# Hybrid retention / MoBA decoder step on one core: the second norm's squares are added on GpSimd before TensorE sums them, and GpSimd's drains give way to semaphore counts

## The chip, the core and the metric

The kernel runs on one core of a Trainium2 chip. A core has TensorE (PE in the profile; PEld is its loading of weights), VectorE (DVE), ScalarE (ACT), GpSimd (POOL), SyncE (SP, which here only issues DMAs) and 16 DMA engines that fill one on-chip memory (SBUF). The metric is the time of one execution on the device in microseconds (us); lower is better.

## The reference, cut to what matters

One decoder layer is applied to a prompt of 512 tokens and to a decoding group of 8 sequences with 4 new tokens each. Model width is 1024, that is 8 tiles of 128 features. All is float32.

```python
h = _rmsnorm(x, norm1_w) * (1 + sc1) + sh1
z = h @ w_in                      # 3584 columns: retention q k v gate, MoBA q k v
...                               # retention and block-sparse attention
x = x + g1 * (concat([ret_out, moba_out]) @ w_out)
h2 = _rmsnorm(x, norm2_w) * (1 + sc2) + sh2     # _rmsnorm: x * rsqrt(mean(x*x) + eps) * w
x = x + g2 * ((silu(h2 @ w_gate) * (h2 @ w_up)) @ w_down)
```

The change touches the second norm of the prompt, whose mean runs over the 1024 features of each token, and the rotary rotation (`x1*cos - x2*sin`, `x1*sin + x2*cos`) of retention queries and keys. The sample group's block-sparse attention reads 8 x 32 pages of cached keys (K) and values (V), 128 rows of 512 numbers each; this is most of the memory traffic and is spread over the whole kernel.

## The kernel before, in words

Every engine has its own hand-written program; they meet at counting semaphores (`s_...`). The work is laid out in numbered slots. Slot `s` holds one group of four pages of the sample's attention, and beside it one piece of the prompt's work.

In slot `s` TensorE first multiplies the turned keys of group `s` with the queries (`keys`, L1161), then does the prompt's piece, then weighs the values of group `s - 12` (`weigh`, L1216). The keys take this way: GpSimd gathers 1 MB of K with an indirect DMA (`gather`, L523) into one of two buffers; VectorE turns it (`turn_keys`, L1846, written KT) when the buffer has arrived and TensorE has used the turned keys before; TensorE uses it in the next slot. `gather(g)` waits until the group `g - 2` is turned, because it takes that buffer. Values come by four DMAs of 256 KB a group, issued by SyncE (L410), into two rings of four buffers; each waits until TensorE has used its buffer.

Slots 13 to 29 hold the last input tiles. There GpSimd also rotates the eight tiles of retention keys and queries (`rotate`, L548, L549, L551): tile `m` at turn `g = m + 4` of its loop, right behind `gather(g)`.

Slots 43 to 50 (`R_OUT + f`, f = 0 to 7) are the ones that the change is about. Output projection tile `f` is 24 matmuls (L1128, L1129, L1130: every product of float32 numbers is made of three rounded ones). For them ScalarE rounds the weights (`split_out`, L658, written whi) and VectorE takes the rest (L1809, written rawlo). When tile `f - 1` is done, VectorE adds it to x (`residual`, L2126), makes the product with the norm's weight (`gained`, L2131), takes `rawlo` for tile `f + 1` (L1809) and turns the next keys (L1846), in this order. ScalarE squares the new x (L950; L961 for the last tile) into one of two buffers `stage`. TensorE sums these squares over the features with a column of ones: `sum_squares(k)`, four matmuls of one column, behind the output tile of the next slot. Four numbers a partition accumulate in PSUM over all eight k, after a product with zeros that clears them (L1548).

In slot 48 VectorE also takes the sums and maxima of a sequence's logits, TensorE forms the gates (`block_gates`, L1180), and VectorE selects the blocks in slot 49 (`select`, L1872 to L1889), ahead of that slot's residual. TensorE's next use of it is `turn_max` (L1184) in slot 49's tail, ahead of the keys of slot 50.

Slot 51 (`R_NORM`) and the two behind it are the norm: VectorE takes the reciprocal (L2160), ScalarE the root, VectorE puts it on four diagonals (L2164), TensorE spreads it over the partitions (L1578), VectorE copies it to `rb` (L2168), GpSimd scales the eight tiles (`scale_x`, L566), ScalarE rounds them (L970), VectorE takes the rest (L2152). Then the feed-forward tiles begin (slot 54 on), and behind slot 64 the sample's own output projection and feed-forward go between them.

GpSimd's program at loop turn `g` is: wait for the turned keys, `gather(g)`, then what that turn holds. At turns 46 and 47 it rotates the sample's queries and keys (`rotate_half`, L532, L533, L535), at turn 48 it masks two blocks of keys (`masked_k`, L541), at turns 54 and 55 it scales the tiles. Between operations that depend on each other it drains its pipe: `pool.drain()`, L534 and L536 in `rotate_half`, L550 and L552 in `rotate`.

Of the kernel before, what the change touches and what calls it, by code (L numbers as in the profile page):

```python
# [7 lines left out]
ALU, ACT, AX = mybir.AluOpType, mybir.ActivationFunctionType, mybir.AxisListType  # L8

P = 128  # L10
# [6 lines left out]
HP = H // 2  # L17
# [9 lines left out]
KT = DM // P  # L27
# [122 lines left out]
def decoder_step(nc, x_prompt, x_sample, cache_k, cache_v, state_ret, page_table, c_prompt, c_sample,  # L150
# [7 lines left out]
    def sem(name):  # L158
        return persist.enter_context(nc.semaphore(name))
# [168 lines left out]
    s_hn, s_sg = sem("heads_normed"), sem("gate_silu")  # L328
    s_kst, s_kss = sem("k_v_prompt_stored"), sem("k_v_sample_stored")

    s_srot, s_srs, s_ssg = sem("s_rotated"), sem("s_rstd"), sem("s_gate_silu")

# [17 lines left out]
    s_le, s_to = sem("logits_kept"), sem("own_probsT_copied")  # L352

    s_sqx, s_ssm, s_r1, s_r2 = sem("x2_squares"), sem("x2_sums"), sem("x2_inverse"), sem("x2_rstd")
    s_nx, s_gmt = sem("x2_scaled"), sem("gmod_turned")

    RINV, RDIAG, RSPREAD = 1, 2, 3
    s_xr, s_x2s, s_x2q, s_x2i = sem("x2T_ready"), sem("x2s_ready"), sem("x2s_squares"), sem("x2s_inverse")
# [161 lines left out]
    def _(pool):  # L520
# [4 lines left out]
        def rotate_half(n, half, op):  # L525
            ta = kmask[0][:, 0:256].rearrange("p (h d) -> p h d", h=H)
            tb = kmask[1][:, 0:256].rearrange("p (h d) -> p h d", h=H)
            cos = C("cos_s").unsqueeze(1).broadcast_to((S, H, 32))
            sin = C("sin_s").unsqueeze(1).broadcast_to((S, H, 32))
            z = zs[:, n * W:(n + 1) * W].rearrange("p (h c d) -> p h c d", h=H, c=2)  # L530
            o = (qrs, krs)[n][:, :].rearrange("p (h c d) -> p h c d", h=H, c=2)
            pool.tensor_tensor(ta, z[:, :, half, :], cos, ALU.mult)  # L532
            pool.tensor_tensor(tb, z[:, :, 1 - half, :], sin, ALU.mult)  # L533
            pool.drain()  # L534
            pool.tensor_tensor(o[:, :, half, :], ta, tb, op)  # L535
            pool.drain()  # L536

        def masked_k(b):
            if b >= 2:
# [4 lines left out]
        def rotate(m):  # L544

            z, other = zT[:, Z_OF[m], :], swapped[:, m % 2, :]
            pool.wait_ge(s_swap[m % 2], 64 * ((m - M_TURN) // 2 + 1))
            pool.tensor_tensor(other, other, C("sin"), ALU.mult)  # L548
            pool.tensor_tensor(z, z, C("cos"), ALU.mult)  # L549
            pool.drain()  # L550
            pool.tensor_tensor(z, z, other, ALU.add)  # L551
            pool.drain().then_inc(s_rk, 1)  # L552

        def queries_decayed(hp):
            if hp == 0:
# [6 lines left out]
        def scale_x(k):  # L562

            if k == 0:
                pool.wait_ge(s_r1, RSPREAD)
            pool.tensor_tensor(zT[:, k, :], zT[:, k, :], rb[:, :], ALU.mult).then_inc(s_nx, 1)  # L566

        def scale_heads(hp):
            pool.wait_ge(s_hrs, hp + 2)
# [7 lines left out]
        for g in range(2, NG):  # L577
            pool.wait_ge(s_kt, g - 1)
            gather(g)
            if M_TURN <= g - 4 < M_TURN + 2 * HP:  # L580
                if g - 4 == M_TURN:
                    pool.wait_ge(s_const, 32)
                rotate(g - 4)
            if g > R_PAIR and (g - R_PAIR - 2) % 3 == 0 and g <= R_PAIR + 11:
                queries_decayed((g - R_PAIR - 2) // 3)
            if g in (R_PAIR + 7, R_PAIR + 10, R_PAIR + 13):
                scale_heads((g - R_PAIR - 7) // 3)
            if g == R_PAIR + 3:
                pool.wait_ge(s_hrs, 1)
                heads = mobatok.rearrange("p i (h d) -> p i h d", h=H)  # L590
                pool.tensor_tensor(heads, heads, gain[:, 4:8, 0:8].unsqueeze(3).broadcast_to((P, TT, H, HD)), ALU.mult).then_inc(s_hm, 1)
            if g in (R_NORM + 3, R_NORM + 4):
                for k in range(4):
                    scale_x(4 * (g - R_NORM - 3) + k)
            if g == R_OUT + 3:
                pool.wait_ge(s_sev, NIN + 2)
                pool.wait_ge(s_xx, KT)
                pool.wait_ge(s_const, 64)
                rotate_half(0, 0, ALU.subtract)
                rotate_half(0, 1, ALU.add)  # L600
            if g == R_OUT + 4:
                rotate_half(1, 0, ALU.subtract)
                rotate_half(1, 1, ALU.add)
                pool.sem_inc(s_srot, 1)
            if g == R_OUT + 5:
                masked_k(0)
                masked_k(1)
            if g == R_SAMPLE + 5:
                pool.wait_ge(s_rpe, SO)
                pool.tensor_tensor(state[:, :, :, :], state[:, :, :, :],  # L610
                                   C("c_dec_s").unsqueeze(1).unsqueeze(3).broadcast_to((P, NB_SEQ, HP, HD)), ALU.mult).then_inc(s_sdc, 1)
            if R_SAMPLE + 6 <= g < R_SAMPLE + 9:
                b = 2 * (g - R_SAMPLE - 5)
                masked_k(b)
                masked_k(b + 1)

    @block.scalar
    def _(act):
# [319 lines left out]
        for f in range(KT):  # L938
# [6 lines left out]
                split_out(f + 1)  # L945
            if f >= 1:
                act.wait_ge(s_ev, F_OUT + f + 2)
                if f >= 3:
                    act.wait_ge(s_ssm, f - 2)
                act.activation(stage[(f - 1) % 2][:, :], x2T[:, f - 1, :], ACT.Square).then_inc(s_sqx, 1)  # L950
            if f == KT - 1:
                exps(B_NORM)
            if f:
# [3 lines left out]

        act.activation(st2[:, 28:29], C("eps"), ACT.Sqrt)
        act.wait_ge(s_ev, F_OUT + KT + 2)
        act.wait_ge(s_ssm, KT - 2)  # L960
        act.activation(stage[1][:, :], x2T[:, KT - 1, :], ACT.Square).then_inc(s_sqx, 1)  # L961
        slot(R_NORM)
        next_chunk(5)
# [20 lines left out]
        def sample_slot(s):  # L984
# [4 lines left out]
            if s == R_SAMPLE + 8:  # L989
                act.wait_ge(s_sts, NB_SEQ // 2)  # L990
                act.dma_start(ret_sample[0].rearrange("b (hp h2) d v -> (h2 d) b hp v", h2=2), state[:, :, :, :]).then_inc(s_state, 16)
                act.wait_ge(s_srot, 1)
                act.dma_start(x2s[:, :], x_sample.rearrange("b t d -> (b t) d")).then_inc(s_xs, 16)
            if s == S_END + 1:
                act.wait_ge(s_ofs, 1)
# [67 lines left out]
    def _(pe):  # L1063
# [479 lines left out]

        def sum_squares(k):
            if k == 0:
                pe.matmul(DB[:, 0:TT], ident, C("pad0")[:, 0:TT], start=True, stop=False, skip_group_check=True)  # L1548
            pe.wait_ge(s_sqx, k + 1)
            for i in range(TT):  # L1550
                last = pe.matmul(DB[:, i:i + 1], stage[k % 2][:, i * P:(i + 1) * P], ones[:, 0:1], start=False, stop=(k == KT - 1),
                                 skip_group_check=True)
            last.then_inc(s_ssm, 1)

        for f in range(KT):
            slot_head(R_OUT + f)
# [7 lines left out]
                 last_in=(lambda: turn_heads(3)) if f == 0 else None)  # L1564
            if f == KT - 1:
                slot_head(R_NORM)
            if f:
                sum_squares(f - 1)
            if f == KT - 1:
                turn_probs(B_NORM, 0)  # L1570
                sum_squares(KT - 1)
            slot_rest(R_OUT + f)


# [40 lines left out]
        def sample_slot(s):  # L1615

            if s == R_SAMPLE:
                pe.wait_ge(s_srot, 1)
                for n, x in enumerate((qrs, krs)):
                    for j in range(HP):  # L1620
                        last = pe.transpose(SB[:, (n * HP + j) * S:(n * HP + j + 1) * S], x[:, j * P:(j + 1) * P], ident[0:S, 0:S])
# [104 lines left out]
    def _(dve):  # L1726
# [429 lines left out]
        residual(KT - 1, 16 + KT - 1, bank[(KT - 1) % 2])  # L2156
        gained(KT - 1)
        turn_half_keys(R_NORM + 1, 0)
        dve.wait_ge(s_ssm, KT)
        then(ts(st2[:, 8:12], DB[:, 0:TT], 1.0 / DM, EPS, ALU.mult, ALU.add))  # L2160
        dve.reciprocal(st2[:, 8:12], st2[:, 8:12]).then_inc(s_r1, 1)
        dve.wait_ge(s_r2, 1)
# [1 line left out]
            last = ts(stage[0][:, i * P:(i + 1) * P], ident, st2[:, i:i + 1], None, ALU.mult)  # L2164
        last.then_inc(s_r1, 1)
        turn_half_keys(R_NORM + 1, 1)
        dve.wait_ge(s_ssm, KT + 1)
        cp(rb[:, :], DB[:, :]).then_inc(s_r1, 1)  # L2168
        slot_head(R_NORM + 1)
        slot_rest(R_NORM + 1)  # L2170
# [238 lines left out]
```

## Time and profile before

| what | value |
|---|---|
| median of 3 runs | 1039.15 us (1037.05 to 1048.32) |
| profiled execution, its own time | 1034.07 us |
| its span, first to last instruction | 1032.2 us |
| TensorE's mean granted clock | 0.976 |
| TensorE busy | 961.6 us, 93% |
| VectorE, ScalarE, GpSimd busy | 624.5, 338.4, 139.4 us |
| DMA | 269.14 MB, mean 261 GB/s |

The profile is of one execution; its time is 5.1 us below the median of the three runs, and 1.9 us above its span. Busy shares are means over stages with different limits. DMA-issuing, semaphore and drain instructions are not counted as busy.

### The profile page before, as it was taken

What the parts mean: (1) busy time and instruction counts of PE and PEld (TensorE: products, weight loads), DVE (VectorE), ACT (ScalarE), POOL (GpSimd) and SP (SyncE); (2) the same over time, 40 slices, a digit from 0 to 9 for tenths busy, and PEclk for the clock granted to TensorE, in tenths of its full rate; (3) what the DMA queues carried; (4) which work ended last, traced back from release to release, by engine and by line L of the source; (5) the groups of instructions that cost most, each with busy time, mean ns of one, the idle gap of its engine ahead of it and who ended that gap; (6) DMA issues with size and microseconds to landing.
All of it is one profiled execution on the core that took longest, in us unless ns stands there. A gap on an engine that the chain in (4) does not pass through costs nothing.

```text
span 1032.2 us, 20974 instructions
## 1 busy us (share of the span) xinstructions
PE 961.6 (93%) x7919; PEld 675.8 (65%) x7919; DVE 624.5 (60%) x1067; ACT 338.4 (33%) x735; POOL 139.4 (14%) x129
## 2 busy tenths in 40 slices
PE   3879998999999987979989999999999999999996
PEld 2557775766666644547756767676777777777775
DVE  1566874677767667876788584432655555453244
ACT  5412233334333624542252152332333222121113
POOL 0011111444210132204151220000000000000000
PEclk9899999999999989999989899999999999999998
DMA  9978877999786889988998668778476988787652
GB/s 340 364 257 282 284 252 268 296 274 300 255 287 215 276 320 390 356 288 280 362 320 285 231 230 265 230 228 267 144 218 167 240 226 231 218 251 248 204 194 87
DMA packets 217973, 269.14 MB, mean 261 GB/s; under 512 B 13473, under 2 KB 168425, under 8 KB 209682
## 3 DMA queue, kind: packets, MB, share of 16 engines
q1 hardware_dynamic: 110226, 126.65, 38.7%
q10 hardware_dynamic: 98432, 74.04, 23.6%
q0 software_dynamic: 9216, 67.11, 17.7%
q8 instruction: 63, 1.03, 0.4%
q14 instruction: 36, 0.29, 0.1%
HBM read 260.04 MB, written 5.64 MB: 257 GB/s over the span
## 4 chain that ended last, share of the span: by engine, by line
PE 72%; DVE 8%; DMA 7%; issue 5%; SPq 4%; DVEq 2%; ACT 1%; POOLq 1%; POOL 1%; ACTq 0%
PE banks L1128 13%; PE banks L1129 12%; PE banks L1130 12%; PE banks L1078 6%; PE banks L1216 4%; PE banks L1141 4%; PE banks L1143 4%; PE banks L1142 4%; PE banks L1161 4%; DVE KT L1846 3%; DMA V<-in_cache_v 3%; DMA K<-in_cache_k,kidx 1%; SPq L420 1%; PE banks L1340 1%; DMA early<-in_w_mod 1%
## 5 line engine op out<-in xcount | busy, mean ns | idle before, releaser
L658 ACT ACTIVATE whi<-raw 128x1024 fp32r<-128x1024 f32 (+1 forms) x76 | 78.6, 1035 | 298.0 <-PE banks L1130 144.4
L1128 PE MATMUL banks<-ahi,whi 128*128 128x512 f32 x416 | 169.2, 407 | 0.1
L1846 DVE STREAM_TRANSPOSE KT<-K 128x2048 f32<-128x2048 f32 x63 | 145.5, 2310 | 30.0 <-DMA K<-in_cache_k,kidx 15.1
L1129 PE MATMUL banks<-alo,whi 128*128 128x512 f32 x416 | 163.5, 393 | 0.0
L1130 PE MATMUL banks<-ahi,rawlo 128*128 128x512 f32 x416 | 163.3, 393 | 0.0
L1809 DVE TENSOR_TENSOR rawlo<-raw,whi 128x1024 fp32r<-128x1024 f32 (+1 forms) x76 | 91.3, 1201 | 54.3 <-ACT whi L658 51.2
L523 POOL DMA_INDIRECT K<-in_cache_k,kidx x64 | 64.0, 1000 | 412.4 <-DVE KT L1846 363.7
L1128 PEld LDWEIGHTS banks<-ahi,whi 128*128 128x128 f32 x416 | 78.7, 189 | 31.2 <-issue 13.1
L1141 PE MATMUL banks<-ahi,whi 128*128 128x512 f32 x216 | 90.2, 417 | 1.2 <-DVE rawlo L1816 0.9
L1130 PEld LDWEIGHTS banks<-ahi,rawlo 128*128 128x128 f32 x416 | 78.8, 189 | 17.3
L1161 PE MATMUL banks<-KT,qbd 128*32 128x128 f32 x2048 | 74.0, 283 | 15.7 <-DVE KT L1846 13.0
L1129 PEld LDWEIGHTS banks<-alo,whi 128*128 128x128 f32 x416 | 78.8, 189 | 14.9
L1143 PE MATMUL banks<-ahi,rawlo 128*128 128x512 f32 x216 | 85.1, 394 | 0.0
L1142 PE MATMUL banks<-alo,whi 128*128 128x512 f32 x216 | 84.9, 393 | 0.0
L1161 PEld LDWEIGHTS banks<-KT,qbd 128*32 128x32 f32 x2048 | 56.7, 112 | 29.7 <-issue 14.1
L1216 PE MATMUL banks<-V,pT 128*32 128x512 f32 x368 | 64.4, 630 | 11.5 <-DMA V<-in_cache_v 11.4
L1816 DVE TENSOR_TENSOR rawlo<-raw,whi 128x1024 fp32r<-128x1024 f32 x28 | 35.8, 1279 | 30.4 <-ACT whi L651 14.9
L1141 PEld LDWEIGHTS banks<-ahi,whi 128*128 128x128 f32 x216 | 40.9, 190 | 17.9 <-issue 7.5
L748 ACT ACTIVATE pm<-banks,st 128x128 f32<-128x128 f32 (+3 forms) x32 | 16.6, 524 | 96.8 <-DVE st L1989 91.4
L1143 PEld LDWEIGHTS banks<-ahi,rawlo 128*128 128x128 f32 x216 | 40.8, 189 | 9.4
L1142 PEld LDWEIGHTS banks<-alo,whi 128*128 128x128 f32 x216 | 41.1, 190 | 7.3
L1750 DVE TENSOR_TENSOR xtmp<-xtmp,banks 32x256 f32<-32x256 f32 x90 | 37.5, 417 | 7.1 <-issue 0.4
(330 smaller groups left out, 1462.1 us busy)
## 6 DMA issues: line engine op xcount, KB each, us to landing
V<-in_cache_v SPq DMA_DIRECT2D x184, 256.0 KB
rawm<-in_w_mod ACTq DMA_DIRECT2D x14, 1024.0 KB
raw<-in_w_in ACTq DMA_DIRECT2D x12, 1024.0 KB
zT<-in_cache_v SPq DMA_DIRECT2D x48, 256.0 KB
raw<-in_w_gate ACTq DMA_DIRECT2D x22, 512.0 KB
raw<-in_w_up ACTq DMA_DIRECT2D x22, 512.0 KB
srw<-in_w_gate SPq DMA_DIRECT2D x22, 512.0 KB, 5.6
srw<-in_w_up SPq DMA_DIRECT2D x22, 512.0 KB, 7.3
```

The lines of the kernel that those rows point to most:

```text
L523: pool.indirect_dma_start(Kb[g % 2][:, :], None, ck, bass.IndirectOffsetOnAxis(kidx[:, g:g + 1], 0)).then_inc(s_k[g % 2], 16)
L658: act.activation(whi[t % 2][:, 0:kd, :], raw[u][:, 0:kd, t % 2 * P:(t % 2 + 1) * P], ACT.Copy).then_inc(s_hi, 1)
L1128: pe.matmul(out[:, :], whi[t % 2][:, k, :], hi(k), start=(first and n == 0), stop=False)
L1129: pe.matmul(out[:, :], whi[t % 2][:, k, :], lo(k), start=False, stop=False)
L1130: last = pe.matmul(out[:, :], low[:, k, :], hi(k), start=False, stop=(final and n == kd - 1))
L1141: pe.matmul(DB[:, :], whi[m % 2][:, k, :], ahi[:, k, :], start=(k == 0), stop=False)
L1142: pe.matmul(DB[:, :], whi[m % 2][:, k, :], alo[:, k, :], start=False, stop=False)
L1143: last = pe.matmul(DB[:, :], wlow[:, k, :], ahi[:, k, :], start=False, stop=(k == KT - 1))
L1161: last = pe.matmul(LG[32 * gq:32 * gq + 32, (g % 4) * P:(g % 4 + 1) * P], qbd[g // NGRP % 2][:, j, :], KTb[:, :, j, :], start=(jj == 0), s ...
L1216: pe.matmul(VO[32 * pg:32 * pg + 32, :], pT[:, n, 32 * pg:32 * pg + 32], bufs[pg][:, :], start=(n == 0), stop=(n == NGRP - 1)).then_inc(s_ ...
L1809: tt(rawlo[u][:, 0:kd, cols], raw[u][:, 0:kd, cols], whi[t % 2][:, 0:kd, :].bitcast(F32), ALU.subtract).then_inc(s_lo, 1)
L1846: dve.transpose(KTb[:, :, :, :], Kb[g % 2][:, :]).then_inc(s_kt, 1)
```

## The change

GpSimd gets a new function, `add_squares(k)`. ScalarE writes the first tile's squares straight into `rb` and the others into `stage` in turn; GpSimd adds tiles 1 to 6 to `rb`, at its loop turns 47 to 52, behind the gather of that turn and ahead of the rotations and masks. TensorE sums twice in all, at the end of slot 50: `rb`, and the last tile's squares. ScalarE's waits for a free `stage` are now for GpSimd (`s_sqa`) and no longer for TensorE (`s_ssm`). In `rotate`, `rotate_half` and before `masked_k` the drains are gone; the operations count one semaphore up (`s_srot`, and `s_rk` from the last operation itself) and GpSimd waits for its count.

```diff
-            pool.tensor_tensor(ta, z[:, :, half, :], cos, ALU.mult)
-            pool.tensor_tensor(tb, z[:, :, 1 - half, :], sin, ALU.mult)
-            pool.drain()
-            pool.tensor_tensor(o[:, :, half, :], ta, tb, op)
-            pool.drain()
+            done = 4 * HP + 3 * (2 * n + half)
+            pool.wait_ge(s_srot, done)
+            pool.tensor_tensor(ta, z[:, :, half, :], cos, ALU.mult).then_inc(s_srot, 1)
+            pool.tensor_tensor(tb, z[:, :, 1 - half, :], sin, ALU.mult).then_inc(s_srot, 1)
+            pool.wait_ge(s_srot, done + 2)
+            pool.tensor_tensor(o[:, :, half, :], ta, tb, op).then_inc(s_srot, 1)
...
-            pool.tensor_tensor(other, other, C("sin"), ALU.mult)
-            pool.tensor_tensor(z, z, C("cos"), ALU.mult)
-            pool.drain()
-            pool.tensor_tensor(z, z, other, ALU.add)
-            pool.drain().then_inc(s_rk, 1)
+            pool.tensor_tensor(other, other, C("sin"), ALU.mult).then_inc(s_srot, 1)
+            pool.tensor_tensor(z, z, C("cos"), ALU.mult).then_inc(s_srot, 1)
+            pool.wait_ge(s_srot, 2 * (m - M_TURN + 1))
+            pool.tensor_tensor(z, z, other, ALU.add).then_inc(s_rk, 1)
...
+        def add_squares(k):
+            pool.wait_ge(s_sqx, k + 1)
+            if k > 1:
+                pool.wait_ge(s_sqa, k - 1)
+            pool.tensor_tensor(rb[:, :], rb[:, :], stage[k % 2][:, :], ALU.add).then_inc(s_sqa, 1)
...
+            if 1 <= g - R_OUT - 3 < KT - 1:
+                add_squares(g - R_OUT - 3)
...
             if g == R_OUT + 5:
+                pool.wait_ge(s_srot, 4 * HP + 12)
                 masked_k(0)
                 masked_k(1)
...
-                if f >= 3:
-                    act.wait_ge(s_ssm, f - 2)
-                act.activation(stage[(f - 1) % 2][:, :], x2T[:, f - 1, :], ACT.Square).then_inc(s_sqx, 1)
+                if f >= 4:
+                    act.wait_ge(s_sqa, f - 3)
+                act.activation(rb[:, :] if f == 1 else stage[(f - 1) % 2][:, :], x2T[:, f - 1, :], ACT.Square).then_inc(s_sqx, 1)
...
-        def sum_squares(k):
-            if k == 0:
-                pe.matmul(DB[:, 0:TT], ident, C("pad0")[:, 0:TT], start=True, stop=False, skip_group_check=True)
-            pe.wait_ge(s_sqx, k + 1)
+        def sum_over_features(src, final):
             for i in range(TT):
-                last = pe.matmul(DB[:, i:i + 1], stage[k % 2][:, i * P:(i + 1) * P], ones[:, 0:1], start=False, stop=(k == KT - 1),
-                                 skip_group_check=True)
-            last.then_inc(s_ssm, 1)
+                last = pe.matmul(DB[:, i:i + 1], src[:, i * P:(i + 1) * P], ones[:, 0:1], start=False, stop=final, skip_group_check=True)
+            return last
+
+        def sum_squares():
+
+            pe.matmul(DB[:, 0:TT], ident, C("pad0")[:, 0:TT], start=True, stop=False, skip_group_check=True)
+            pe.wait_ge(s_sqa, KT - 2)
+            sum_over_features(rb, False)
+            pe.wait_ge(s_sqx, KT)
+            sum_over_features(stage[1], True).then_inc(s_ssm, 1)
...
             if f == KT - 1:
                 slot_head(R_NORM)
-            if f:
-                sum_squares(f - 1)
             if f == KT - 1:
                 turn_probs(B_NORM, 0)
-                sum_squares(KT - 1)
+                sum_squares()
```

The other edits renumber waits to fit: the last square waits for `s_sqa >= 5`, VectorE for `s_ssm` 1 and 2, and TensorE's and ScalarE's waits for the rotated sample rows are now `s_srot >= 28`.

## Rows read from the trace of the kernel before

**Rows 1.** The page, part 1: busy time, share of the span and instructions.

```profile
PE 961.6 (93%) x7919; PEld 675.8 (65%) x7919; DVE 624.5 (60%) x1067; ACT 338.4 (33%) x735; POOL 139.4 (14%) x129
```

**Rows 2.** Busy time by window (start:end us, length; engines; clock; DMA share; GB/s).

```profile
503.00:512.00 9.00, 9.00 (x76) 6.92 (x76) 5.73 (x19) 1.06 (x1) 0.94 (x1) 1.00 1.00 346
...
531.00:545.00 14.00, 9.80 (x81) 4.37 (x73) 13.76 (x12) 7.28 (x13) 11.53 (x10) 0.76 1.04 388
```

**Rows 3.** Line L1551, all instructions: count, min/median/max ns, first and last start.

```profile
L1551 PE MATMUL banks<-ct,stage x64: 164/250/271, 470.5 to 527.2; 128*128 128x1 f32 x64
```

**Rows 4.** TensorE's instructions in order of time (start, length, then what).

```profile
479.51 0.95 PE L1551 MATMUL banks<-ct,stage 128*128 128x1 f32 x8
480.38 1.07 PE L1216 MATMUL banks<-zT,pT 128*32 128x512 f32 x8
```

**Rows 5.** The chain that ended last, 451 to 500 us (start, length, what).

```profile
477.67 7.83 issue
...
489.52 6.85 DMA K<-in_cache_k,kidx
...
496.40 2.32 DVE KT L1846
...
498.85 1.08 PE banks L1161 x32
```

**Rows 6.** GpSimd's instructions in order of time, around the sample's rotations.

```profile
475.05 1.16 POOL L523 DMA_INDIRECT K<-in_cache_k,kidx  x1 [0.78 <-issue]
...
476.92 0.74 POOL L533 TENSOR_TENSOR kmask<-zs,cts 32x256 f32<-32x256 f32 x1
485.53 0.73 POOL L535 TENSOR_TENSOR krs<-kmask,kmask 32x256 f32<-32x256 f32 x1 [7.86 <-issue]
```

**Rows 7.** VectorE's instructions in order of time, slots 45 to 49.

```profile
467.77 2.30 DVE L1846 STREAM_TRANSPOSE KT<-K 128x2048 f32<-128x2048 f32 x1
...
485.38 2.31 DVE L1846 STREAM_TRANSPOSE KT<-K 128x2048 f32<-128x2048 f32 x1 [1.02 <-DMA K<-in_cache_k,kidx]
...
513.18 1.22 DVE L1809 TENSOR_TENSOR rawlo<-raw,whi 128x1024 fp32r<-128x1024 f32 x1
514.32 2.31 DVE L1846 STREAM_TRANSPOSE KT<-K 128x2048 f32<-128x2048 f32 x1
```

**Rows 8.** TensorE's instructions in order of time, slots 47 to 50.

```profile
497.64 1.07 PE L1216 MATMUL banks<-zT,pT 128*32 128x512 f32 x8
...
508.09 0.39 PE L1180 MATMUL banks<-sm,ct 128*128 128x16 f32 x2
...
516.87 0.27 PE L1184 MATMUL banks<-ct,sm 128*1 128x128 f32 x1
517.07 1.08 PE L1161 MATMUL banks<-KT,qbd 128*32 128x128 f32 x32
```

**Rows 9.** ScalarE's instructions in order of time: the square of tile 5.

```profile
512.72 0.64 ACT L950 ACTIVATE stage<-x2T 128x512 f32<-128x512 f32 x1 [4.12 <-DVE x2T L2126]
```

**Rows 10.** Line L566, all instructions: GpSimd's operation on one tile of 128x512.

```profile
L566 POOL TENSOR_TENSOR zT<-zT,rb x8: 1259/1268/1280, 531.4 to 541.5; 128x512 f32<-128x512 f32 x8
```

**Rows 11.** ScalarE in order of time: the first tile rounded behind GpSimd's scaling.

```profile
532.71 0.72 ACT L970 ACTIVATE ahi<-zT,mT 128x512 fp32r<-128x512 f32 x1 [3.94 <-POOL zT L566]
```

**Rows 12.** In order of time, VectorE and GpSimd: operations that overlap, near 252 us.

```profile
251.97 1.91 DVE L1816 TENSOR_TENSOR rawlo<-raw,whi 128x1024 fp32r<-128x1024 f32 x1 [2.32 <-ACT whi L651]
...
252.76 2.25 POOL L549 TENSOR_TENSOR zT<-zT,ctr 128x512 f32<-128x512 f32 x1
```

**Rows 13.** GpSimd in order of time: the first rotation of a prompt tile.

```profile
182.84 1.28 POOL L551 TENSOR_TENSOR zT<-zT,swapped 128x512 f32<-128x512 f32 x1 [1.55 <-issue]
```

**Rows 14.** TensorE in order of time, the norm's slots: values awaited, first feed-forward matmul.

```profile
534.50 2.45 PE L1216 MATMUL banks<-V,pT 128*32 128x512 f32 x4 [2.41 <-DMA V<-in_cache_v]
...
544.58 0.50 PE L1128 MATMUL banks<-ahi,whi 128*128 128x512 f32 x1
```

**Rows 15.** Line L2152, all instructions: VectorE's rest of the eight scaled tiles.

```profile
L2152 DVE SCALAR_TENSOR_TENSOR alo<-zT,mT,ahi x8: 737/740/5524, 535.2 to 545.9; 128x512 fp32r<-128x512 f32 x8
```

More of the change, by code:

```diff
@@ L329, in decoder_step @@
     s_kst, s_kss = sem("k_v_prompt_stored"), sem("k_v_sample_stored")
-    s_srot, s_srs, s_ssg = sem("s_rotated"), sem("s_rstd"), sem("s_gate_silu")
+    s_srot, s_srs, s_ssg = sem("rotation_steps"), sem("s_rstd"), sem("s_gate_silu")
     s_rpe, s_rdve = sem("s_retention_on_pe"), sem("s_retention_on_dve")
@@ L354, in decoder_step @@
     s_sqx, s_ssm, s_r1, s_r2 = sem("x2_squares"), sem("x2_sums"), sem("x2_inverse"), sem("x2_rstd")
-    s_nx, s_gmt = sem("x2_scaled"), sem("gmod_turned")
+    s_nx, s_gmt, s_sqa = sem("x2_scaled"), sem("gmod_turned"), sem("x2_squares_added")
     RINV, RDIAG, RSPREAD = 1, 2, 3
@@ L603, in _ @@
                 rotate_half(1, 1, ALU.add)
-                pool.sem_inc(s_srot, 1)
             if g == R_OUT + 5:
+                pool.wait_ge(s_srot, 4 * HP + 12)
                 masked_k(0)
@@ L959, in _ @@
         act.wait_ge(s_ev, F_OUT + KT + 2)
-        act.wait_ge(s_ssm, KT - 2)
+        act.wait_ge(s_sqa, KT - 3)
         act.activation(stage[1][:, :], x2T[:, KT - 1, :], ACT.Square).then_inc(s_sqx, 1)
@@ L991, in sample_slot @@
                 act.dma_start(ret_sample[0].rearrange("b (hp h2) d v -> (h2 d) b hp v", h2=2), state[:, :, :, :]).then_inc(s_state, 16)
-                act.wait_ge(s_srot, 1)
+                act.wait_ge(s_srot, 4 * HP + 12)
                 act.dma_start(x2s[:, :], x_sample.rearrange("b t d -> (b t) d")).then_inc(s_xs, 16)
@@ L1617, in sample_slot @@
             if s == R_SAMPLE:
-                pe.wait_ge(s_srot, 1)
+                pe.wait_ge(s_srot, 4 * HP + 12)
                 for n, x in enumerate((qrs, krs)):
@@ L2158, in _ @@
         turn_half_keys(R_NORM + 1, 0)
-        dve.wait_ge(s_ssm, KT)
+        dve.wait_ge(s_ssm, 1)
         then(ts(st2[:, 8:12], DB[:, 0:TT], 1.0 / DM, EPS, ALU.mult, ALU.add))
@@ L2166, in _ @@
         turn_half_keys(R_NORM + 1, 1)
-        dve.wait_ge(s_ssm, KT + 1)
+        dve.wait_ge(s_ssm, 2)
         cp(rb[:, :], DB[:, :]).then_inc(s_r1, 1)
```

## The prediction

> **What bounds the kernel now.** I read the page first. TensorE is busy 93% of the span, VectorE 60%, GpSimd 14% [rows 1]. Such a kernel gets shorter by what leaves TensorE, as long as nothing else comes late, and the page cannot say whether something does. So I went to the stretch that the change touches, slots 44 to 51 (about 464 to 531 us), by windows. From 503 to 512 us TensorE is busy for the whole of 9.00 us at a granted clock of 1.00 [rows 2]. The same row shows the DMA engines at a share of 1.00 and 346 GB/s, so they are the second candidate. Behind the norm it is different: from 531 to 545 us TensorE works 9.80 of 14.00 us, its mean granted clock is 0.76, and the DMA share is 1.04 [rows 2].
>
> Then the chain that ended last. Just where TensorE is full, this chain runs over GpSimd: 7.83 us of "issue", then a gather's transfer of 6.85 us, the turning of its keys, and at 498.85 us TensorE's keys [rows 5]. GpSimd's own timeline tells what that "issue" is: between L533 at 476.92 us and L535 at 485.53 us stands only the drain L534, 7.86 us long [rows 6]. VectorE's wait for the preceding gather (issued 475.05 us) ends at 485.38 us [rows 7]. So in this trace the drain ends when the outstanding gather lands. A chain says who was last, not by how much: before the keys at 498.85 us TensorE's previous group starts at 497.64 us and takes 1.07 us [rows 8], which leaves 0.14 us. Both paths are almost equally long there.
>
> **The sums on TensorE.** L1551 has 64 records, 8 for each of 8 groups [rows 3]. Busy times overlap, so I take start to start: the group at 479.51 us is followed by the values at 480.38 us, 0.87 us [rows 4]. Six of eight groups go: 6 x 0.87 = 5.22 us, all on the engine that is full. The clearing product moves from the first to the last group, and nets to nothing. At the end of slot 50 there are two sums as before, in a slightly different order around the turned probabilities, so the way from the last tile to the norm is not shortened. All the gain must come from slots 44 to 49.
>
> **The drains of the sample's rotations.** Without them, gather 47 can go when group 45 is turned, at 467.77 + 2.30 = 470.07 us [rows 7], and not at 475.05 us; gathers 48 and 49 move up by more, since 7.86 us of drain lie behind the first. Their keys stop being late, which is worth the 0.14 us above, and keeps this path from being the next bound when TensorE gets faster: with the drains left, the 3.5 us of the first four groups would be lost against it. The new waits count GpSimd's own operations. They could hang on the outstanding gather like the drains, or cost next to nothing. ScalarE's first rounding starts at 532.71 us [rows 11], 0.05 us after the first scaling (531.4 + 1.26 us [rows 10]) ended, with a gather issued just ahead of it; so an operation's count comes at once. I take 0; the other end is a rival.
>
> **The drains of the prompt's rotations.** The first has 1.55 us of drain before L551 [rows 13], and there are two a tile. Sixteen at up to 1.55 us are 25 us of GpSimd, which is 14% busy [rows 1]. That idle time is the cover: the rotated tiles are needed slots later, and a gather mostly waits for turned keys longer than for this. Were the cover gone, a gather would come up to 3.1 us later in each of eight slots. I take 0, since no stretch of the chain that I read there runs over these drains.
>
> **The additions on GpSimd.** Six operations of 128x512, 1.27 us each by the nearest operation of that size [rows 10], 7.6 us of an engine with room. ScalarE's new waits are for additions at least a slot old: 0. The wait that counts is on GpSimd: `add_squares(k)` waits for the square of tile k, and behind it in GpSimd's queue stand the rotations, the masks and the next gather. For tile 5 the square ends at 512.72 + 0.64 = 513.36 us [rows 9], so the addition ends near 514.7 us. The next gather waits for a group of keys whose turning begins at 514.32 us and takes 2.31 us [rows 7]. So the gather's own condition comes 2 us later, and the addition delays nothing. In slot 50 tile 6's square gives the same order. I take 0, up to 0.5 us a slot if ScalarE were late.
>
> **Contention with VectorE.** The addition starts when VectorE does `rawlo`, which is on the way to the next turned keys. Near 252 us such a pair overlaps: `rawlo` takes 1.91 us and GpSimd's product 2.25 us, and not about 1.22 and 1.28 us [rows 7, 10, 12]. So they hold each other. For tile 5, `rawlo` starts at 513.18 us, 0.18 us ahead of the square's end; then GpSimd is the one that waits, and it has time. In slot 50 `exp_bias` comes between and the addition may be first, which costs up to 1.27 us in that slot. Bounds: 0, and 1.27 us in each of the three last slots (3.8 us). I take 0.2 us, near the lower end, since five of six slots have the order of tile 5.
>
> The Trainium skill (SBUF — State Buffer, "Who interferes with whom") says that a VectorE instruction with two SBUF inputs contends with a GpSimd instruction that reads SBUF, and that the first to issue holds the port for its whole length. The trace agrees. The rule speaks against this change; with GpSimd first in every slot it gives the slow rival below.
>
> **What is late next.** TensorE gains 0.87 us a slot only while keys are ready. The tight place is slot 50: from `block_gates` at 508.09 us to the keys at 517.07 us TensorE takes 8.98 us [rows 8], 8.11 us without the sum. VectorE starts on the gates' result and has turned the keys at 514.32 + 2.31 = 516.63 us, 8.54 us after the same point, and 0.14 us more pass until TensorE uses them (as at 498.71 to 498.85 us [rows 5]): 8.68 us. So 8.68 - 8.11 = 0.57 us are given back. I found no second place so tight, with slot 51's keys next.
>
> **The sum.** -5.22 - 0.14 + 0.57 + 0.2 = -4.6 us. Behind the norm each load starts upon a use by TensorE, so the whole pattern shifts earlier, waits included. Against the profiled execution: 1034.07 - 4.6 = 1029.5 us. The median of the runs is 5.1 us above that execution, so against it 1034.5 us. The measurement tells about 1% (10.4 us) from no change; this is 0.4%.
>
> **The rivals.**
>
> *The transfers absorb it.* With the DMA share at 1.00 [rows 2] a faster TensorE may only wait for bytes. For: 346 to 388 GB/s in these windows. Against: a slot moves 2.5 MB (1 of K, 1 of V, half a weight chunk of 1), which in a slot of 8.11 us is 308 GB/s, below the 388 GB/s of the second row of [rows 2]. If it held, gain 0: 1039.2 us.
>
> *More is gained at the norm.* The first feed-forward matmul, at 544.58 us, waits behind values (2.41 us at 534.50 us [rows 14]). VectorE's last rest starts at 545.9 us and takes 0.74 us [rows 15], 546.6 us, and is needed only by the last three of 24 matmuls. Slot 49's 8.98 us less gates, keys, sum, values and turned maximum (0.3, 1.0, 0.9, 1.0, 0.2) leave 5.6 us for a tile, so 21 matmuls take 4.9 us, and a start at 541.7 us would do. If earlier gathers clear the queues, up to 2.9 us more: 1031.6 us. Against: those values are requested upon TensorE's use, also after the change.
>
> *GpSimd first, slower than before.* In every slot the addition starts ahead of `rawlo` and holds it 1.27 us, keys follow late, and 7.6 us are paid against 5.36 gained: +7.6 + 0.57 - 5.36 = +2.8 us, 1042.0 us. It decides once the uncovered hold is over (5.36 - 0.57) / 6 = 0.8 us a slot. Against: the order at 513 us, and the idle time that VectorE has in most slots (5.73 us busy of 9.00 [rows 2]).
>
> *The stall stays.* The change doesn't free GpSimd, because its counts too wait for the gather. Then the four first groups' 3.5 us and an addition's 1.27 us are lost on the way to gather 48: -4.6 + 3.5 + 1.3 = about 0, 1039.3 us. Against: rows 11.
>
> **How the numbers follow.** Forecast 0.60, absorbed 0.12, more at the norm 0.13, GpSimd first 0.10, stall 0.05. The forecast's own range is 1032 to 1038.5 us (no contention; contention at its upper bound). The range must take in the slow rival at 1042 and the better one, and three runs before spread from 1037.05 to 1048.32 us, so medians move by a few us: 1029 to 1042 us. No case reaches 1% by its terms; faster by over 1% gets 0.06 (the norm's waits shrinking with a better clock), slower by over 1% 0.04, within 1% 0.90.
>
> **What would show it.** Right: L1551's successor has 16 records; no "issue" over 1 us before L535; gather 48 issued before 480 us; slots 44 to 49 shorter by about 0.87 us each save one, where the keys of slot 50 wait for VectorE some 0.5 us; first feed-forward matmul 4.6 us earlier. Wrong: `rawlo` at 2 us or more in these slots, additions that end after the turned keys, or new waits for K, V or weights between 464 and 531 us.

## The result, and the profile after

The changed kernel takes 1045.2 us (median of 20 runs, 1042.3 to 1049.76), the kernel before 1040.59 us (20 runs, 1034.26 to 1049.24). The measured ratio is 1.0052, with a 95% interval of 1.0032 to 1.0073. That is 5.4 us slower (the two medians alone differ by 4.6 us), and not 4.6 us faster. It is within 1%, and 1045.2 us is above the end of my range (1042 us).

The two profiled executions stand at opposite ends of their spreads: that of before took 1034.07 us, less than any of the 20 runs, that of after 1049.76 us, the longest of its 20 (span 1047.9 us). Already at the keys of slot 44, ahead of the second norm's part of the change, they are 9.7 us apart (463.73 and 473.41 us). So I compare stretches from one TensorE landmark to the next, and no absolute times.

The page, part 1, of after; it answers to [rows 1]:

```profile
PE 961.3 (92%) x7871; PEld 672.0 (64%) x7871; DVE 624.7 (60%) x1067; ACT 338.3 (32%) x735; POOL 152.3 (15%) x135
```

48 matmuls are gone and six GpSimd operations have come, as meant. GpSimd in order of time, after, slots 44 to 49; it answers to [rows 6]:

```profile
480.56 0.98 POOL L525 DMA_INDIRECT K<-in_cache_k,kidx  x1 [0.38 <-DVE KT L1859]
483.44 1.81 POOL L575 TENSOR_TENSOR rb<-rb,stage 128x512 f32<-128x512 f32 x1 [1.91 <-ACT stage L961]
485.21 0.73 POOL L536 TENSOR_TENSOR kmask<-zs,cts 32x256 f32<-32x256 f32 x1
485.91 0.72 POOL L537 TENSOR_TENSOR kmask<-zs,cts 32x256 f32<-32x256 f32 x1
486.72 0.73 POOL L539 TENSOR_TENSOR krs<-kmask,kmask 32x256 f32<-32x256 f32 x1
...
489.89 0.98 POOL L525 DMA_INDIRECT K<-in_cache_k,kidx  x1 [0.16 <-issue]
...
495.53 0.98 POOL L525 DMA_INDIRECT K<-in_cache_k,kidx  x1 [0.16 <-issue]
...
502.83 0.95 POOL L525 DMA_INDIRECT K<-in_cache_k,kidx  x1 [1.33 <-DVE KT L1859]
```

The "issue" of 7.86 us ahead of `krs` is gone: the second of its products (L537) ends at 486.63 us and L539 starts at 486.72 us. In after the trace has no landing for the gather issued at 480.56 us, but in e9, a second profile of the same kernel, the same gather goes at 479.25 us and lands 9.5 us later, at 488.7 us, while the first L539 for `krs` starts at 485.41 us. So the counts don't wait for the gather. From gather 46 (473.54 us here, 463.85 us before) to gather 48 it takes 16.35 us, and before 25.67 us. Up to here all goes as predicted, and TensorE takes it up: its keys start as follows, in order of time (the last two are those of slots 48 and 49):

```profile
481.54 1.06 PE L1172 MATMUL banks<-KT,qbd 128*32 128x128 f32 x32
...
489.56 1.08 PE L1172 MATMUL banks<-KT,qbd 128*32 128x128 f32 x32
...
504.80 1.26 PE L1172 MATMUL banks<-KT,qbd 128*32 128x128 f32 x32
512.08 1.07 PE L1227 MATMUL banks<-V,pT 128*32 128x512 f32 x8
520.57 0.61 PE L1191 MATMUL banks<-sm,ct 128*128 128x16 f32 x2 [7.43 <-DVEq L1880]
521.11 1.94 PE L1172 MATMUL banks<-KT,qbd 128*32 128x128 f32 x32
```

From the keys of slot 44 to those of slot 48 (473.41 to 504.80 us) it takes 31.39 us, and before 35.12 us: 3.73 us gained. The next slot takes 16.31 us, and before 9.56 us. TensorE ends its values at 513.15 us and stands for 7.43 us until the gates can be taken. The chain that ended last, after, 495 to 522 us, says why:

```profile
496.36 17.00 DMA raw<-in_w_out
...
513.38 1.06 ACT whi L669
...
514.64 3.27 DVEq L1874
517.91 1.10 DVE sm L1872
519.01 1.12 DVE sm L1873
```

The last chunk of `w_out` (1 MB, the weights of tiles 6 and 7) is 17.00 us under way. ScalarE, which rounds it, and VectorE, which takes its rest ahead of everything else, each in order of time:

```profile
496.36 0.39 ACTq L831 DMA_DIRECT2D raw<-in_w_out  x1
...
513.38 1.06 ACT L669 ACTIVATE whi<-raw 128x1024 fp32r<-128x1024 f32 x1 [13.60 <-DMA raw<-in_w_out]
```

```profile
514.47 1.23 DVE L1822 TENSOR_TENSOR rawlo<-raw,whi 128x1024 fp32r<-128x1024 f32 x1 [9.11 <-ACT whi L669]
515.61 2.31 DVE L1859 STREAM_TRANSPOSE KT<-K 128x2048 f32<-128x2048 f32 x1
517.84 1.18 DVE L1872 TENSOR_REDUCE sm<-lgs 128x8 f32<-128x1024 f32 x1
```

One late load holds three things that don't need it: VectorE works in its written order, so behind `rawlo` stand the turning of keys (gathered from 495.53 us on; in e9 this gather landed in 8.9 us) and both reductions for the gates, and behind these TensorE. In the kernel before, this chunk was issued at 488.53 us and its rounding began at 497.03 us, released by TensorE and not by the load: it was there within 8.5 us.

The windows of after and of before (start:end, length, busy times as in [rows 2], granted clock, DMA share, GB/s):

```profile
486.00:508.00 22.00, 22.00 (x230) 16.07 (x229) 13.26 (x21) 3.87 (x5) 12.72 (x12) 1.00 1.05 368
508.00:514.00 6.00, 5.14 (x27) 3.23 (x25) 0.00 (x0) 0.62 (x1) 0.00 (x0) 1.00 0.81 309
514.00:522.00 8.00, 1.43 (x22) 1.33 (x26) 6.58 (x10) 1.90 (x3) 2.74 (x2) 0.62 0.94 305
```

```profile
486.00:508.00 22.00, 21.75 (x206) 16.54 (x204) 16.12 (x22) 4.33 (x6) 8.32 (x10) 1.00 0.93 342
```

The DMA engines are full for 22 us on end (a share of 1.05), and the rate over the same 22 us rises from 342 to 368 GB/s. The last row of after shows a second price: behind the stop the granted clock is 0.62, a mean of the two levels 1.2 and 2.4 GHz, and the keys at 521.11 us take 1.94 us and not 1.08. The following slot, 521.11 to 531.33 us, takes 10.22 us, and the same slot before took 8.66 us.

The view of DMA issues, after and before (queue, count, KB of a descriptor or a load, median us from issue to landing); both loads go through ScalarE's queue, the state's first:

```profile
state<-in_state_ret ACTq DMA_DIRECT2D x1, 0.2 KB, 17.8
```

```profile
state<-in_state_ret ACTq DMA_DIRECT2D x1, 0.2 KB, 11.8
```

The state (1 MB, issued at 480.83 us) lands at 498.6 us, 2.2 us after the chunk was issued behind it; before, it was issued at 471.17 and landed at 483.0 us, 5.5 us ahead of the chunk.

### The profile page after: what moved, and what is told of

The parts are those of the page before. It is cut to its first block, busy times and chain, and to the rows that moved or that the text cites. A ratio compares the mean times of both kernels' runs of the same rounds, so it can differ in the third digit from the quotient of the medians.

```text
span 1047.9 us, 20865 instructions
## 1 busy us (share of the span) xinstructions
PE 961.3 (92%) x7871; PEld 672.0 (64%) x7871; DVE 624.7 (60%) x1067; ACT 338.3 (32%) x735; POOL 152.3 (15%) x135
## 4 chain that ended last, share of the span: by engine, by line
PE 69%; DMA 12%; DVE 10%; SPq 2%; issue 2%; DVEq 2%; ACT 1%; ACTq 0%; POOLq 0%
PE banks L1139 14%; PE banks L1140 12%; PE banks L1141 12%; PE banks L1089 6%; PE banks L1227 5%; DMA V<-in_cache_v 4%; DVE KT L1859 4%; PE banks L1152 4%; PE banks L1172 4%; DMA K<-in_cache_k,kidx 3%; PE banks L1154 3%; PE banks L1153 3%; DMA early<-in_w_mod 2%; DMA raw<-in_w_out 2%; PE banks L1351 1%
## 5 line engine op out<-in xcount | busy, mean ns | idle before, releaser
L1227 PE MATMUL banks<-V,pT 128*32 128x512 f32 x368 | 67.5, 643 | 16.7 <-DMA V<-in_cache_v 16.7
```

What stands on the lines that cost most here:

```text
L1227: pe.matmul(VO[32 * pg:32 * pg + 32, :], pT[:, n, 32 * pg:32 * pg + 32], bufs[pg][:, :], start=(n == 0), stop=(n == NGRP - 1)).then_inc(s_ ...
```

## The experiments

Each kernel has 12 runs. They fall into three groups (e1 to e4, e5 to e8, e9 to e12), each with 35 runs of the kernel before on the same chip (medians 1038.57, 1040.07 and 1040.22 us), and the ratios are against these. The table gives what I read from each profile, in us. "Chunk" is the last one of `w_out`, from issue to its rounding; with a "<" its landing was earlier, since TensorE released the rounding (where the trace has that landing, it is 5.0 us after the issue in e3 and 5.6 us in e7). "State" is from issue to landing; "moved" where it is loaded later. The last time column runs from the keys of slot 44 to the first feed-forward matmul.

| kernel | keys 44 to 48 | 48 to 49 | chunk | state | 44 to feed-forward | ratio (95%) |
|---|---|---|---|---|---|---|
| before | 35.12 | 9.56 | < 8.5 | 11.8 | 80.85 | 1 |
| changed | 31.39 | 16.31 | 17.0 | 17.8 | 86.85 | 1.0052 (1.0032 to 1.0073) |
| e9, changed again | 31.37 | 16.82 | 17.5 | 18.2 | 84.48 | 1.0051 (1.0022 to 1.008) |
| e1, additions only | 37.35 | 10.98 | < 8.1 | 15.8 | 83.24 | 1.0022 (0.9992 to 1.0052) |
| e2, sample's counts only | 34.76 | 9.14 | 11.3 | 19.6 | 81.83 | 1.0022 (0.9997 to 1.0048) |
| e3, prompt's counts only | 35.47 | 9.19 | < 8.5 | 11.0 | 81.42 | 0.9992 (0.9967 to 1.0018) |
| e4, gather 49 held | 31.37 | 15.05 | 10.4 | 17.5 | 82.47 | 1.0037 (1.0014 to 1.006) |
| e5, state later | 31.37 | 9.67 | 10.6 | moved | 75.60 | 0.9988 (0.9956 to 1.0019) |
| e6, before, state later | 34.78 | 10.76 | 13.2 | moved | 82.07 | 1.0008 (0.9978 to 1.0037) |
| e7, before, six sums out | 36.69 | 11.09 | < 9.0 | 16.2 | 83.24 | 1.0038 (1.0005 to 1.0072) |
| e8, before, additions on top | 35.69 | 9.16 | < 8.5 | 12.5 | 81.21 | 1.0016 (0.9987 to 1.0045) |
| e10, e5 again | 31.41 | 8.37 | < 7.7 | moved | 74.65 | 0.9989 (0.996 to 1.0019) |
| e11, values held | 31.36 | 10.48 | 10.5 | 19.0 | 78.13 | 1.0004 (0.9974 to 1.0033) |
| e12, both | 31.38 | 9.17 | 9.3 | moved | 76.30 | 0.9966 (0.9939 to 0.9993) |

### The parts of the change, each alone

**e1: the additions, with all drains back.** Against the changed kernel:

```diff
...
-            pool.wait_ge(s_srot, done + 2)
-            pool.tensor_tensor(o[:, :, half, :], ta, tb, op).then_inc(s_srot, 1)
+            pool.drain()
+            pool.tensor_tensor(o[:, :, half, :], ta, tb, op)
+            pool.drain()
```

and the same in `rotate`.

> The additions on GpSimd and the two sums on TensorE as in the change; all drains as before. Collision theory (the sample's rotations without drains send gathers 48 to 50 early, into the load of w_out's last chunk, which then takes 17.0 us and stops TensorE for 7.4 us): without that, no stop; gathers 47 to 49 are late as before, so most of the six sums' 5.2 us is lost against them: ratio 0.997 to 1.001. Additions theory (waits and port contention of the additions cost the time): ratio 1.004 or more, as in the full change. Prompt theory (the counts in the prompt's rotations cost it, upstream): ratio below 1.000.

1042.83 us. With TensorE faster the gathers are late, each engine in order of time (GpSimd, VectorE, TensorE):

```profile
485.44 0.73 POOL L535 TENSOR_TENSOR kmask<-zs,cts 32x256 f32<-32x256 f32 x1
492.44 0.73 POOL L537 TENSOR_TENSOR krs<-kmask,kmask 32x256 f32<-32x256 f32 x1 [6.28 <-issue]
...
496.42 0.98 POOL L525 DMA_INDIRECT K<-in_cache_k,kidx  x1 [0.80 <-issue]
```

```profile
505.30 2.31 DVE L1859 STREAM_TRANSPOSE KT<-K 128x2048 f32<-128x2048 f32 x1 [4.31 <-DMA K<-in_cache_k,kidx]
```

```profile
507.76 1.93 PE L1172 MATMUL banks<-KT,qbd 128*32 128x128 f32 x32 [5.34 <-DVE KT L1859]
```

The gather behind the drains takes 8.9 us to land (6.85 us in [rows 5]), and TensorE stands for 5.34 us. So the time that TensorE gave up comes back as this wait, and more: 37.35 us against 35.12. The chunk is in time here. The ratio of 1.0022 lies between the two theories, above the 1.001 of the one and below the 1.004 of the other, and its interval touches both; it is the trace that tells the late gathers from a cost of the additions.

**e2: the counts of the sample's rotations alone.** Against before, only `rotate_half` and the waits for it take the change's form, with 3 counts a half and 12 in all.

> Only the sample's rotations (rotate_half) get counts in place of drains; sums, additions and the prompt's rotations as before. Collision theory: the gathers go early and the load of w_out's last chunk takes over 12 us to land, with nothing gained on TensorE: slower, ratio 1.005 to 1.010, and an idle time of several us on TensorE in slot 48 or 49. Additions theory: 1.000. Prompt theory: 1.000.

1041.03 us. The gathers go early, the state takes 19.6 us, and the rounding of the chunk is the first that waits for the load. ScalarE in order of time:

```profile
504.50 1.06 ACT L659 ACTIVATE whi<-raw 128x1024 fp32r<-128x1024 f32 x1 [7.06 <-DMA raw<-in_w_out]
```

It starts 11.3 us after the issue at 493.24 us, and TensorE, still with its sums to do, has no wait in slot 48 or 49. So the expectation was too hard: the chunk took less than 12 us, there was no idle time, and the ratio is 1.0022 and not 1.005 or more. Taking the drains away thus moved the lateness from K to the weights and the state, ahead of any gain.

**e3: the counts of the prompt's rotations alone.** Against before, only `rotate` takes the change's form.

> Only the prompt's rotations (rotate) get counts in place of drains. Collision theory and additions theory: nothing, ratio 0.999 to 1.001; the 4 to 5 us by which the changed kernel's profile is late from slot 17 to 24 are the spread between executions. Prompt theory: ratio 1.003 to 1.005, and the same lag from slot 17 on in the profile.

1039.23 us, ratio 0.9992: nothing, as predicted for this part. Its profile does lag from slot 15 on (keys at 195.4 us, before 189.9 us), but so do e1, e6, e7 and e8, which keep these drains (193.8 to 195.4 us); the lag is no mark of the counts. It is the one profile of before that is early.

**e8: the additions on top of before.** TensorE's eight sums stay; GpSimd does the six additions as well, and ScalarE waits for both.

```diff
+            if 1 <= g - R_OUT - 3 < KT - 1:
+                add_squares(g - R_OUT - 3)
...
                     act.wait_ge(s_ssm, f - 2)
+                    act.wait_ge(s_sqa, f - 2)
```

> The kernel before with all eight groups of sums on TensorE, and the six additions on GpSimd besides (their result is not used). All drains as before. Transfer theory: the additions are free but for the turns behind the drains, up to 2.6 us at gather 48 and 49, ratio 1.000 to 1.003. Additions theory: 1.004 or more.

1039.97 us, ratio 1.0016; the stretch to the feed-forward differs by 0.4 us. The additions as such cost nothing that these runs resolve.

**e7: the first six sums left out of before, and nothing in their place.**

```diff
         def sum_squares(k):
-            if k == 0:
+            if k == KT - 2:
                 pe.matmul(DB[:, 0:TT], ident, C("pad0")[:, 0:TT], start=True, stop=False, skip_group_check=True)
...
-            if f:
+            if f == KT - 1:
                 sum_squares(f - 1)
```

> The kernel before with the first six groups of sums left out and nothing in their place: the norm's mean misses six of eight tiles. No additions; all drains as before. Transfer theory: TensorE's 5.2 us are turned into waits for keys or weights in slots 47 to 49, ratio 0.999 to 1.003. Additions theory: the full 5 us appear, ratio 0.995 to 0.997.

1043.6 us, ratio 1.0038: slower than with the work. VectorE, then TensorE:

```profile
503.99 2.31 DVE L1843 STREAM_TRANSPOSE KT<-K 128x2048 f32<-128x2048 f32 x1 [3.06 <-DMA K<-in_cache_k,kidx]
```

```profile
494.86 1.08 PE L1158 MATMUL banks<-KT,qbd 128*32 128x128 f32 x32 [1.11 <-DVE KT L1843]
506.45 1.93 PE L1158 MATMUL banks<-KT,qbd 128*32 128x128 f32 x32 [3.85 <-DVE KT L1843]
```

5.2 us of TensorE's work are gone, and the waits of 1.11 and 3.85 us and a slot at the lower clock take their place. This is the study's plainest run: there is no addition and no count in it, and still the gain isn't there. From the keys of slot 44 to those of slot 50 e7 takes 56.04 us, 2.7 us more than before, though its two waits add up to 4.96 us only. The keys at half speed (1.93 us) are part of the difference; the rest I can't account for. Its ratio is also just above the 1.003 that the transfer theory gave.

### The transfers, with all of the change in place

**e9: the changed kernel again**, beside e10 to e12.

> The changed kernel itself, on the same chip as the three that follow. Ratio 1.003 to 1.007; w_out's last chunk lands over 12 us after its issue and TensorE stops for several us in slot 48. If the first profile was only one bad execution (rival: the stop is chance), the load lands within 11 us and no wait over 3 us stands in slots 47 to 49.

1045.87 us, and the same stop. ScalarE, then TensorE, in order of time:

```profile
495.04 0.39 ACTq L831 DMA_DIRECT2D raw<-in_w_out  x1
...
512.58 1.06 ACT L669 ACTIVATE whi<-raw 128x1024 fp32r<-128x1024 f32 x1 [14.12 <-DMA raw<-in_w_out]
```

```profile
519.77 0.61 PE L1191 MATMUL banks<-sm,ct 128*128 128x16 f32 x2 [7.93 <-DVEq L1880]
```

Two executions give 7.43 and 7.93 us, so it is a trait of this kernel and not of one run.

**e4: gather 49 waits for the chunk.**

```diff
             pool.wait_ge(s_kt, g - 1)
+            if g == R_OUT + 6:
+                u, loaded = w_buffer(3)
+                pool.wait_ge(s_w[u], loaded)
             gather(g)
```

> The full change, but gather 49 waits until the last chunk of w_out has landed. Collision theory: the load lands within 10 us of its issue, TensorE's 7.4 us of idle time in slot 48's tail is gone, and the time falls below the kernel before: ratio 0.994 to 0.998. Additions theory and prompt theory: as the full change, 1.005.

1044.78 us, ratio 1.0037 and not 0.994 to 0.998: as a way out of the loss it failed. The chunk lands in 10.4 us and not in 17, so the early gather had been in its way. But then the held K is late, as VectorE and TensorE show:

```profile
513.26 2.31 DVE L1862 STREAM_TRANSPOSE KT<-K 128x2048 f32<-128x2048 f32 x1 [3.51 <-DMA K<-in_cache_k,kidx]
```

```profile
518.24 0.61 PE L1194 MATMUL banks<-sm,ct 128*128 128x16 f32 x2 [6.39 <-DVEq L1883]
```

One wait is traded for another, since both loads are needed within the same slot. Here, right behind a gather, the addition at 507.37 us takes 1.29 us, and `rawlo` beside it 3.03 us and not 1.22.

**e5 and e10: the state, 1 MB, is loaded in slot 54.** Nothing needs it in slots 45 to 50.

```diff
-            if f == 2:
+            if s == R_SAMPLE:
                 act.wait_ge(s_vd, 4 * 32)
                 act.dma_start(state[:, :, :, :], state_ret[0].rearrange("b (hp h2) d v -> (h2 d) b hp v", h2=2)).then_inc(s_state, 16)
```

> The full change, and the 1 MB load of the retention state (issued at slot 45, 11.8 us to land before) moved behind the norm, to slot 54. Transfer theory (the DMA engines are busy nearly all the time from slot 45 to 50, so w_out's last chunk or a gather comes late whatever TensorE saves): with 1 MB less there, the stop of 6 to 7 us in slot 48 shrinks below 3 us and the kernel comes 3 us or more below the change: ratio 0.996 to 1.002 against the kernel before. Additions theory: no change, 1.005.

> The change with the state's load in slot 54, on the same chip as the change. Transfer theory: 3 to 6 us faster than the preceding run, ratio 0.997 to 1.000 against the kernel before. Chance: the same as the preceding run within 2 us.

1039.57 and 1041.53 us, ratios 0.9988 and 0.9989. The chunk lands in 10.6 us, and in less than 7.7 us in e10. In e5 TensorE's wait at the gates is down from 7.43 us; ScalarE, then TensorE:

```profile
504.89 1.06 ACT L669 ACTIVATE whi<-raw 128x1024 fp32r<-128x1024 f32 x1 [7.17 <-DMA raw<-in_w_out]
```

```profile
512.10 0.39 PE L1191 MATMUL banks<-sm,ct 128*128 128x16 f32 x2 [1.22 <-DVEq L1880]
512.42 1.08 PE L1172 MATMUL banks<-KT,qbd 128*32 128x128 f32 x32
...
520.68 1.08 PE L1172 MATMUL banks<-KT,qbd 128*32 128x128 f32 x32 [0.32 <-DVE KT L1859]
```

In e10 there is no wait at the gates at all. Against the changed kernel of its own group e10 is 4.3 us shorter by the medians, and the penalty is gone. Neither ratio can be told from 1, so nothing is gained over the kernel before either.

**e6: the same move in the kernel before.**

> The kernel before with the same move of the state's load. Transfer theory: TensorE was full in these slots with only 0.14 us to spare, so 1 MB less gives at most 1 us: ratio 0.998 to 1.001, and the preceding run (the change with the move) at or below it. Additions theory: the preceding run stays 4 us or more above this one.

1040.59 us, ratio 1.0008: nothing, so the move is no gain in itself. Its chunk took 13.2 us even without the state, and TensorE waited 1.55 us at the gates (515.76 us), a small form of the same stop in a kernel without the change. So the state is one of several loads in the chunk's way and not the cause alone.

**e11: a group of values waits for the chunk instead.**

```diff
+            if g == 36:
+                u, loaded = w_buffer(3)
+                sp.wait_ge(s_w[u], loaded)
```

> The full change with the state's load where it was; the values of group 36, otherwise issued about 2 us behind w_out's last chunk, wait until that chunk has landed. Transfer theory: the chunk shares the engines with one queue less and lands within 12 us; the stop in slot 48 falls from 7 to 1 to 4 us: ratio 0.999 to 1.004. Chance: as the change, with the values late on top, 1.005 to 1.008.

1040.25 us, ratio 1.0004. The state still takes 19.0 us, and yet the chunk lands in 10.5 us, with no wait for it at TensorE's gates. The values are only needed some slots later, so holding them costs little; TensorE waits 0.31 us for one at 504.85 us. So the stop goes when either of two other loads is out of the way.

**e12: both, values held and state later.**

> Both: the state's load in slot 54 and the values of group 36 held. Transfer theory: no wait for weights is left in slots 47 to 49, TensorE's 5 us are kept: ratio 0.995 to 0.998, faster than the kernel before. Chance: 1.000 to 1.005.

1037.89 us, ratio 0.9966 (0.9939 to 0.9993): faster than both kernels, 3.5 us by the ratio. ScalarE, then TensorE:

```profile
503.68 1.06 ACT L672 ACTIVATE whi<-raw 128x1024 fp32r<-128x1024 f32 x1 [5.93 <-DMA raw<-in_w_out]
```

```profile
511.63 0.40 PE L1194 MATMUL banks<-sm,ct 128*128 128x16 f32 x2
511.96 1.08 PE L1175 MATMUL banks<-KT,qbd 128*32 128x128 f32 x32
```

The gates have no wait. What this run doesn't show is how much of the 3.5 us is the change's: the kernel before with both moves was not run, only with the state's (e6, nothing). The interval ends just below 1, and it overlaps those of e10 and e5.

## Why the prediction was wrong

**TensorE's share: right.** The four slots in which nothing is late gain 3.73 us; by 0.87 us a sum and the 0.14 us of late keys I had 3.62 us. The same 31.4 us stand in every profile with the whole change.

**The sample's drains: right.** They lasted as long as the outstanding gather, the counts don't, and gather 48 goes 9.3 us earlier after gather 46, where I had expected at least 9.5 us (ahead of 480 us, from 489.52 us). "With the drains left, the 3.5 us would be lost" was right as well, and too kind: e1 loses 2.2 us beyond them.

**The prompt's drains, and the additions: right.** e3 shows nothing, e8 nothing that can be told from no change. `rawlo` takes 1.21 to 1.23 us in the slots of after that I read, where my slow rival had the addition go first and hold it. What is held is the addition: 1.29 to 2.18 us over the six, median 1.97 us, and not 1.27. The Trainium skill (SBUF — State Buffer, "Who interferes with whom") says that the two share a port pair under an exclusive lock; the trace agrees in the five slots in which `rawlo` starts first and keeps its own time. In slot 50 the addition may be first, as I had reckoned: in after VectorE's 128x8 operation at 533.57 us takes 1.34 us beside it, and before 0.23 us. It costs TensorE nothing to be seen: e5 has this hold and e10 doesn't, and from the keys of slot 50 to those of slot 51 they take 6.98 and 7.07 us. GpSimd-first in every slot, the rival that I gave for a slower kernel, is refuted as the cause of this one.

**What is late next: wrong, and this is the step that failed.** I looked for the next tight place only among VectorE's turned keys, and found slot 50 (0.57 us; where the stop is gone the profiles show 0.32 us at 520.68 us in e5). The waits for weights I put at nothing, without a term in the sum and without a reason: I never asked by how much these loads were in time, though I named new waits for weights as a sign of being wrong. In its place the runs showed a chunk 17.0 us under way, TensorE standing for 7.43 us, and a slot that is 6.75 us longer. All that the trace proved of the chunk was that it came within 8.5 us, on a queue with a 1 MB load ahead of it, in a stretch at a DMA share near 1.00. Of K, V, the state and the chunk, three moved: the gathers by up to 9 us through the drains, V and the chunk with TensorE's uses. They met.

**"The transfers absorb it": dismissed by a sum that was wrong.** I set 2.5 MB a slot against 388 GB/s. The state's 1 MB was missing from it, though its load lies in slot 45. From 486 to 508 us 8.1 MB moved, 2.9 MB for each of 2.8 slots of 7.8 us; in the 8.11 us of my sum that would be 354 GB/s and not 308, no longer well below the 346 to 388 GB/s that these windows reached. And such a mean says nothing of order. Even so the rival would have given 1039.2 us, no gain. The actual cost is larger, because the loads did not land in the order of need: the state, needed much later, was under way until 498.6 us, and the chunk until 513.4 us. The Trainium skill (DMA: Bandwidth & Descriptors, "Issuing engines are not separate DMA queues") says that loads issued from SyncE, ScalarE and GpSimd run on the same 16 DMA engines and interleave; the trace agrees, with a chunk that takes 17.0 us beside gathers, values and the end of the state, and under 8.5 us beside gathers that come late.

**The sum, corrected.** From the keys of slot 44 to those of slot 50: 3.7 us gained in four slots, 6.75 us lost in the fifth, 1.56 us in the sixth, together +4.6 us (57.92 against 53.34 us). Behind it the norm's slots take 1.4 us more (28.93 against 27.51 us). That is +6.0 us by these two profiles; by e9, the other profile of the changed kernel, it is +3.6 us (84.48 against 80.85 us). The runs give 5.4 us by the ratio, so single profiles fit its size only roughly. Behind the first feed-forward matmul both take the same 487.6 us.

**Shown and not shown.** Shown: the stop and its releaser (two executions), that the additions and the prompt's counts don't cause it (e8, e3, and e10, which has both and no wait at the gates), that it goes when the state or the values are out of the chunk's way (e5, e10, e11), and that the change with both moves is faster than before (e12). Not settled are four points. First, e5 and e10 shorten the stretch to the feed-forward by 5.3 and 6.2 us against before, and the ratios are lower by some 1 us only. The keys of slot 44 start at 470.8 us on average over the seven profiles with the whole change, and at 468.7 us over the seven others (each kind has one near 464 us). The difference stands in slot 36, ahead of the second norm, where TensorE waits for values, as here in after:

```profile
417.35 2.59 PE L1227 MATMUL banks<-V,pT 128*32 128x512 f32 x4 [2.24 <-DMA V<-in_cache_v]
```

That slot takes 9.9 to 12.2 us in six of the seven profiles with the whole change (6.6 us in e11), and 7.2 to 10.3 us in the others. I found no cause, and the ranges overlap. Second, how much of e7's loss is a wait and how much the clock. Third, which of gather, values and state delays the chunk by how much: no run has varied the gathers alone with K in time. Fourth, whether the kernel before would gain by both moves too.

## What to carry to other kernels

Before counting a gain on the busiest engine, list each load that lands in the stretch, with its need time and the time by which the trace proves it there; a load whose margin is unknown is a bound, not a nothing. Where the DMA engines' share is near 1, as it was here, taking a stall from an issuing engine may only change who is late (e2); try first to move out a load that nobody needs soon (here the state). Look also at what stands in program order behind an operation that waits for a load: here one rounding held a turning of keys and two reductions, and so TensorE for 7.43 us.

## What the runs showed of the hardware

- In these traces GpSimd's drain behind an indirect DMA lasted until that DMA had landed: 7.86 us in [rows 6] and 6.28 us in e1, and in e7 the gather landed at 492.46 us and the next operation started at 492.64 us. Counts on the operations themselves didn't: 0.1 us between them with a gather outstanding (e9).
- The same 1 MB load (the last chunk) on the same queue took 5.0 us (e3) to 17.5 us (e9), with different loads under way beside it.
- The state's load, in rows of 0.2 KB, took 11.0 to 12.5 us beside late gathers and 17.5 to 19.6 us beside early ones; with the sums out but the drains left it lay between, 15.8 and 16.2 us.
- Taking 5.2 us of matmuls out of a busy TensorE (e7) made the kernel some 4 us slower (ratio 1.0038, 1.0005 to 1.0072). After a wait of 3.85 us the keys took 1.93 us, and after waits of 5 to 8 us the same; after one of 1.22 us they took 1.08 us, at full clock.
